# Wide projection fills of the first block queued on TensorE in halves of 12 products instead of whole

## The reference, cut to what matters

```python
h = rmsnorm(x, gain)
u = h @ w_in                      # all projections: q, k, v, z, merge gates
y0 = gated_delta_rule(q, k, v, beta, g)      # GDN, chunks of 64 tokens
y1 = gated_linear_attention(...)             # GLA, 4 heads
y2 = ssd(...)                                # SSD, state-space scan
y3 = sparse_attention(...)                   # NSA: compressed, selected and window keys
for n in range(4):
    y = norm(y_n) * silu(z_n)
    merged += sigmoid(u_gate_n) * (y @ w_br[n])
x = x + merged @ w_out
```

## Time and the profile before

| what | value |
|---|---|
| time, median of 3 runs | 2018.33 us (2018.2 to 2020.39) |
| the profiled execution | 2024.89 us, span 2023.1 us |
| instructions | 28936 |
| mean granted TensorE clock | 0.972 of full speed |
| TensorE busy | 1914.2 us, 95% of the span |
| DVE, ACT, POOL busy | 757.7, 652.8, 543.2 us |
| block one's branches GDN, GLA, SSD, NSA | about 101 to 272, 272 to 490, 490 to 640, 640 to 883 us |
| merge and w_out, block two | 883 to 953, 953 to 2023 us |

### The profile page before, as it was taken

One profiled execution on the slowest core, in us unless ns is written; L12 is line 12 of the kernel. 1 busy time (PEld: TensorE's weight loads), 2 busy tenths in 40 slices (PEclk: granted clock), 3 DMA queues, 4 the chain that ended last, 5 costly groups with the idle time before them and its releaser, 6 DMA issues. The chain is left out here.

```text
span 2023.1 us, 28936 instructions
## 1 busy us (share of the span) xinstructions
PE 1914.2 (95%) x11837; PEld 1438.9 (71%) x11837; DVE 757.7 (37%) x1500; ACT 652.8 (32%) x1251; POOL 543.2 (27%) x420
## 2 busy tenths in 40 slices
PE   6999899998999999999999999999979999999997
PEld 4788877777888777777787887987775444444442
DVE  4367462244322323323434135143242343343333
ACT  4542333232223444435344246343332111111110
POOL 2242233235553433158045230252200000000000
PEclk9999999999899999999999999999989999999999
DMA  5230121124124200252133221232148999999994
GB/s 158 63 88 24 43 73 62 42 63 125 32 63 126 63 22 22 63 194 73 42 123 110 76 81 37 67 102 84 42 201 315 417 413 415 419 418 419 420 420 174
DMA packets 133209, 313.40 MB, mean 155 GB/s; under 512 B 15296, under 2 KB 103120, under 8 KB 108496
## 3 DMA queue, kind: packets, MB, share of 16 engines
q1 hardware_dynamic: 133072, 311.49, 41.3%
HBM read 309.37 MB, written 2.10 MB: 154 GB/s over the span
## 5 line engine op out<-in xcount | busy, mean ns | idle before, releaser
L321 POOL TENSOR_TENSOR unit_low<-unit_ring,unit_high 128x512 fp32r<-128x512 f32 x332 | 437.0, 1342 | 779.2 <-ACT unit_high L314 779.2
L358 PE MATMUL dense<-hT,unit_high 128*128 128x512 f32 x656 | 270.5, 412 | 3.0 <-DVE dense_temps L473 1.7
L359 PE MATMUL dense<-hT,unit_high 128*128 128x512 f32 x656 | 260.4, 397 | 0.0
L360 PE MATMUL dense<-hT,unit_low 128*128 128x512 f32 x656 | 259.8, 396 | 0.0
L396 PE MATMUL dense<-unit_high,hT 128*128 128x256 f32 x832 | 242.5, 291 | 0.4 <-POOL unit_low L321 0.4
L397 PE MATMUL dense<-unit_low,hT 128*128 128x256 f32 x832 | 237.6, 286 | 0.0
L398 PE MATMUL dense<-unit_high,hT 128*128 128x256 f32 x832 | 237.5, 286 | 0.0
L314 ACT CAST unit_high<-unit_ring 128x512 fp32r<-128x512 f32 x332 | 185.8, 620 | 57.3 <-PE dense L360 28.3
L396 PEld LDWEIGHTS dense<-unit_high,hT 128*128 128x128 f32 x832 | 161.9, 195 | 8.0 <-ACT mix_v L2785 3.0
L397 PEld LDWEIGHTS dense<-unit_low,hT 128*128 128x128 f32 x832 | 161.9, 195 | 0.9 <-issue 0.7
L398 PEld LDWEIGHTS dense<-unit_high,hT 128*128 128x128 f32 x832 | 161.7, 194 | 0.0
(11 more groups left out here) (578 smaller groups left out, 3218.0 us busy)
## 6 DMA issues: line engine op xcount, KB each, us to landing
expert_ring<-w_exp_gate SPq DMA_DIRECT2D x64, 1024.0 KB, 9.7
expert_ring<-w_exp_up SPq DMA_DIRECT2D x64, 1024.0 KB, 10.5
expert_ring<-w_exp_down SPq DMA_DIRECT2D x64, 1024.0 KB, 9.0
unit_ring<-w_in SPq DMA_DIRECT2D x55, 1024.0 KB, 5.3
unit_ring<-w_br SPq DMA_DIRECT2D x16, 512.0 KB, 6.3
unit_ring<-w_mkv SPq DMA_DIRECT2D x8, 1024.0 KB, 5.4
x<-x SPq DMA_DIRECT2D x8, 512.0 KB, 4.8
w_out_raw<-w_out SPq DMA_DIRECT2D x4, 1024.0 KB, 10.0
```

Of the source, the lines that this page charges most:

```text
L321: nc.gpsimd.tensor_tensor(low[:, at:at + 512], raw[:, at:at + 512], high[:, at:at + 512], ALU.subtract).then_inc(*self.split.up())
L358: nc.tensor.matmul(out, high[:, k, c], rh, start=(k == 0), stop=False)
L359: nc.tensor.matmul(out, high[:, k, c], rl, start=False, stop=False)
L360: last = nc.tensor.matmul(out, low[:, k, c], rh, start=False, stop=(k == kd - 1))
```

## The change

The fills of block one, and the one kind of block two that shares `dense_z`, yield in the middle: `channels_by_half` after 4 of 8 slices (12 products of 512 columns), `tokens_by_half` after the first of the bank's two token tiles (24 products of 256 columns). Merge products (12) stay whole. `weave` counts in halves: what is due grows by twice `counts[i]` behind each narrow step, half of what is due (rounded up) is issued there, and the rest is carried to the next steps. Everywhere else `fill(dense)` advances to the end of a fill as `next(dense)` did. Casts and evacuation are still issued after the fill's last product. No product, copy or DMA is added or left out; only the order changes (and ACT has two more loads of its function table, in GDN's scores). TensorE's wide work then stands in 165 runs between narrow products instead of 147.

```diff
+    def channels_by_half(self, n, part, col, src, kd=KD, after=None):
...
+        self.round_rest(n)
...
+        for ks in (range(kd // 2), range(kd // 2, kd)):
+            @self.core.section.tensor
+            def _(pe):
+                if ks.start == 0:
+                    if self.free[b]:
+                        pe.wait_ge(*self.free[b])
...
+                for k in ks:
+                    if col == 0:
+                        pe.wait_ge(*self.ready[n, part, k])
...
+                if ks.stop == kd:
+                    last.then_inc(*self.filled.up())
+            if ks.start == 0:
+                yield HALF
+        return self.bank[b], self.filled.now(), b
...
     for c in range(2):
-        got = ring.channels(n, 0, c * P, S.hT)
+        got = yield from ring.channels_by_half(n, 0, c * P, S.hT)
...
-            got = ring.tokens(n, (2 * f, 2 * f + 1), S.hT)
+            got = yield from ring.tokens_by_half(n, (2 * f, 2 * f + 1), S.hT)
...
-                next(dense)
+                fill(dense)
...
+def fill(fills, *over):
+
+    while next(fills, *over) == HALF:
+        pass
+
+
 def weave(steps, fills, counts):
 
+    due, begun = 0, False
     for i, _ in enumerate(steps):
-        for _ in range(counts[i] if i < len(counts) else 0):
-            next(fills, None)
+        due += 2 * counts[i] if i < len(counts) else 0
+        now = (due + 1) // 2
+        while now > 0:
+            half = next(fills, None) == HALF
+            size = 1 if half or begun else 2
+            begun, now, due = half, now - size, due - size
```

More of the change, by code:

```diff
@@ L227, in band_of @@
     return table[:, at:at + n]
+HALF = "half"
 def placed(core, name, offset, shape, dt=F32):
@@ L362, in channels @@
         return self.fill(emit, after)
+    def channels_by_half(self, n, part, col, src, kd=KD, after=None):
+        nc = self.core.nc
+        self.round_rest(n)
+        high, low = self.parts(n, part)
+        b = self.fills % 2
+        self.fills += 1
+        out, c = self.bank[b][:], slice(col, col + P)
+        for ks in (range(kd // 2), range(kd // 2, kd)):
[4 more added lines that the diff above has]
+                        pe.wait_ge(*self.free[b])
+                    if after:
+                        pe.wait_ge(*after)
+                for k in ks:
+                    if col == 0:
+                        pe.wait_ge(*self.ready[n, part, k])
+                    rh, rl = src[:, 0, k, :], src[:, 1, k, :]
+                    nc.tensor.matmul(out, high[:, k, c], rh, start=(k == 0), stop=False)
+                    nc.tensor.matmul(out, high[:, k, c], rl, start=False, stop=False)
+                    last = nc.tensor.matmul(out, low[:, k, c], rh, start=False, stop=(k == kd - 1))
+                if ks.stop == kd:
[3 more added lines that the diff above has]
+        return self.bank[b], self.filled.now(), b
@@ new lines, in tokens_by_half, with _ @@
+    def tokens_by_half(self, n, tiles, src):
+        nc = self.core.nc
+        self.round_rest(n)
+        high, low = self.parts(n, 0)
+        b = self.fills % 2
+        self.fills += 1
+        for i, t in enumerate(tiles):
+            @self.core.section.tensor
+            def _(pe):
+                if i == 0 and self.free[b]:
+                    pe.wait_ge(*self.free[b])
+                out, s = self.bank[b][:, i * 256:(i + 1) * 256], slice(t * P, (t + 1) * P)
+                for k in range(KD):
+                    if t == 0:
+                        pe.wait_ge(*self.ready[n, 0, k])
+                    nc.tensor.matmul(out, src[:, 0, k, s], high[:, k, :], start=(k == 0), stop=False)
+                    nc.tensor.matmul(out, src[:, 0, k, s], low[:, k, :], start=False, stop=False)
+                    last = nc.tensor.matmul(out, src[:, 1, k, s], high[:, k, :], start=False, stop=(k == KD - 1))
+                if i == 1:
+                    last.then_inc(*self.filled.up())
+            if i == 0:
+                yield HALF
+        return self.bank[b], self.filled.now(), b
@@ L550, in dense_merge @@
             chunk = 2 * i + c
-            gate = ring.channels(unit, 0, c * P, S.hT)
+            gate = yield from ring.channels_by_half(unit, 0, c * P, S.hT)
             ring.round(3)
@@ L1627, in dense_ssd_x @@
     for i in range(2):
-        for _ in dense_conv(core, ring, S, f"ssd_x{i}", taps, bias, 2 * i, lambda c: xT[:, c, :], temps, False):
+        for got in dense_conv(core, ring, S, f"ssd_x{i}", taps, bias, 2 * i, lambda c: xT[:, c, :], temps, False):
+            if got == HALF:
+                yield HALF
+                continue
             if chunk >= 1:
@@ L1638, in turn @@
         _, S.ssd_ready = turn_chunk(core, S, bT[:, g, :], S.chunk["ssd_b", g], Bt[:, :, g * P:(g + 1) * P])
[L1639 to L1640 removed]
+    yield from dense_conv(core, ring, S, "ssd_b", taps, bias, 4, lambda c: bT[:, c, :], temps, False)
     turn(0)
[L1642 to L1643 removed]
+    yield from dense_conv(core, ring, S, "ssd_c", taps, bias, 6, lambda c: cT[:, c, :], temps, False)
     turn(1)
@@ L1684, in dense_nsa_kv @@
         n = ring.at[name]
-        got = ring.channels(n, 0, 0, S.hT)
+        got = yield from ring.channels_by_half(n, 0, 0, S.hT)
         ring.round(2)
@@ L1688, in dense_nsa_kv @@
         yield
-        got = ring.channels(n, 0, P, S.hT)
+        got = yield from ring.channels_by_half(n, 0, P, S.hT)
         ring.round(2)
@@ L2442, in blocks @@
         for i in range(8):
-            next(inputs)
+            fill(inputs)
             next(delta)
@@ L2575, in blocks @@
         for i, (k, half) in enumerate(pieces):
-            next(dense, None)
+            fill(dense, None)
             cols = slice(half * SEQ, (half + 1) * SEQ)
```

## The result

The changed kernel takes 2031.2 us (median of 4, 2029.97 to 2031.87), the kernel before 2018.26 us (median of 4): 12.9 us slower, ratio 1.007 with a 95% interval of 1.0048 to 1.0092. The forecast was 2011.8 us, faster; the time lies outside the range, on the other side.

A forecast was written before the change was run, and what follows sets the result against it. TensorE, busy 95% of the span, bounds the kernel, so only its gaps and clock can win. GDN +3.7, GLA +3.1, NSA +1.5 and switches -1.8 make 6.5 us off 2018.3: 2011.8 us, range 2003 to 2020.5.

The forecast's parts named there:

- The step that failed: Closing condition for being wrong: ScalarE's casts, issued later, might leave fills waiting for weights; counted at nothing.
- Nothing to tell: Rival: waits only move and GLA's clock stays low; 0.6 us gained, 2017.7 us; chance 0.25.
- The slower rival: Shorter wide blocks in NSA lower its clock from 0.97 to 0.92, costing 12.2 us; 2024.0 us; chance 0.12.
- GDN, the last tile's state: A half now stands ahead of the state's read, covering its wait of 1.55 us: +1.6 us.
- GDN, the wait for a ring bank: Turnings between halves shorten the 1.7 us wait for a bank the convolution reads: +0.7 us, bounds 0 and +1.7.
- GDN, v and the first inversions: Halves cover up to 2.8 us of waits, less 1.1 new behind the last z evacuation: +1.7, bounds 0 and +2.8.
- GDN, the first solve: Only a half now covers the scaling before the first solve: -0.3 us, from 0 to 1.7 lost.
- GLA, the factors of the last tile: The 3.51 us stall falls to about 0.3, as the tanh moves behind ScalarE's copies: +3.2 us, or +2.1.
- GLA, the clock behind the stall: Without the last tile's stall, the low clock in the fill after it goes: +1.6 us, bounds 0 and +1.6.
- GLA, the new wait: SSD's second turning of B waits behind GLA's last outputs for VectorE's state update, 1.4 to 1.9 us: -1.7.
- NSA: Four of 16 waits for the softmax's maximum get a half in front: +1.5 us, upper bound +4.2.
- Switches: Each of 18 additional pieces of wide work costs 0.1 us: -1.8 us, bounds 0 and -3.6.

The follow-up runs named there:

- casts at the half: Changed kernel with the next unit's casts issued between a fill's two halves instead of after the second, everywhere; 2014.74 us against 2018.04 for the kernel before.
- the two pairs of casts mended: Changed kernel with only two pairs of GDN's casts put back ahead of the exponentials, between the halves; 2017.88 us against 2019.28 for the kernel before.
- the swap in GLA: On casts at the half, the fourth fill ahead of GLA's weave moved behind the turning of the first tile's factors; 2021.29 us, 1.0016 of the kernel before.
- whole fills with late casts: Kernel before, with two pairs of GDN's casts issued one narrow step later, behind the exponentials; 2036.63 us, ratio 1.0093 to the kernel before.
- GDN's table: On casts at the half, GDN's halves set by hand ahead of its waits; 2005.15 us against 2018.55 for the kernel before, ratio 0.9935.

## Why the prediction was wrong

**The step that failed** is the one named last and counted at nothing: "if ACT's casts, now issued later, leave fills waiting for their weights [...] for which I have counted nothing". The rival *Nothing to tell* had it again as "the casts of the next unit now start later", as an argument and without a price. I had shown on ScalarE's order what the change does to a tanh that stands ahead of copies, and did not ask the same of the casts that move with it. In GDN it cost 3.99 + 3.87 = 7.9 us of waits, and the stage went from one stretch of 3.4 us at 1.2 GHz to five of some 24 us together; in all 15.2 us of the stage, by the run with casts at the half. The chain could be read from the order: casts behind L828, L828 behind VectorE's decays, these behind the scores, and between the scores and the product that needs the casts only half a fill and twelve products of the next, 4.4 us.

**The slower rival was the wrong one.** It put the loss in NSA by the clock. NSA's clock stayed at 0.97, with 32 pieces of wide work for 22. The clock did matter, but in GDN, above all at two waits of 4 us.

**GDN, the last tile's state:** +1.6 forecast, 4.7 to 3.1 us measured. Right.

**GDN, the wait for a ring bank:** +0.7 forecast, 1.7 to 0.8 us measured. Right.

**GDN, v and the first inversions:** +1.7 forecast. The waits of 1.2 and 1.6 us went, a new one of 2.3 us came, where I had 1.1: about 0.5 us is left. The mechanism, a gate evacuation ahead of the weighing, was right, its price too low by half.

**GDN, the first solve:** -0.3 forecast, no wait in the changed kernel, 1.8 us with casts at the half, 0.6 with the two pairs of casts mended; so within the bounds of 0 and 1.7 or just beyond. As reckoned, the scaling's operation of 1.79 us took 0.69 in the changed kernel, where no cast runs beside it.

**GLA, the factors of the last tile:** +3.2 forecast; the line went from 7.7 to 4.3 us, this stall from 3.51 to 0.23. Right. But 4.1 us, 1.4 each, for the other three was a wrong reading of a row of totals. The longest, 3.6 us, was not this stall but the one at the first tile, which the change left at 3.6, and the two between were 0.3 each:

```profile
302.06 0.42 PE L1351 MATMUL core<-ident,factors 128*64 128x128 f32 x1 [3.61 <-ACT factorsT L1358]
```

**GLA, the clock behind the stall:** +1.6 forecast, 0 measured. The low stretch at 419 us went, and one of the same length came at 449 us, right behind the new wait:

```profile
449.05 1.00 PE L1667 MATMUL core<-ident,ssd_BT 128*128 128x128 f32 x4 [1.32 <-DVE state L1478]
```

**GLA, the new wait:** -1.7 forecast, 1.32 us measured, in the place and on the operation named. Right, a little under its bounds of 1.4 to 1.9, but for the clock behind it.

**NSA:** +1.5 forecast, 8.4 to 7.7 us measured, in 12 waits as forecast ("some twelve waits"). The four that went are the four counted (0.56, 0.38, 0.28 and 0.26, together 1.5 us), but two others grew by 0.35 and 0.42 us, from 0.29 and 0.51 us in the kernel before:

```profile
776.71 0.49 PE L1870 MATMUL core<-nsa_kwT,nsa_qT 64*128 64x256 f32 x2 [0.29 <-DVE neg_max L1881]
838.85 0.30 PE L1870 MATMUL core<-kcmpT,nsa_qT 64*128 64x31 f32 x2 [0.51 <-DVE neg_max L1881]
```

to 0.64 and 0.93 us in the changed kernel:

```profile
786.67 0.49 PE L1930 MATMUL core<-nsa_kwT,nsa_qT 64*128 64x256 f32 x2 [0.64 <-DVE neg_max L1941]
851.05 0.30 PE L1930 MATMUL core<-kcmpT,nsa_qT 64*128 64x31 f32 x2 [0.93 <-DVE neg_max L1941]
```

Each of these two stands one or two narrow steps behind a half that the change put among the steps. So part of what was covered seems to have been passed on to a later wait, as the rival *Nothing to tell* had it in its words ("Waits only move"); no run takes this apart.

**Switches:** -1.8 forecast. NSA has ten more pieces and lost 0.7 us of waits, and its window is 0.5 shorter, so ten pieces cost 0.2 us; both profiles have the same 13.6 us at 1.2 GHz in the stage. Nearly nothing, not 0.1 to 0.2 each. The row of 2.95 us shows a surplus of 0.2 at a piece's edges; that narrow products among themselves pay only half of it stood in no row. The Trainium skill's rule ("TensorE: Matmul & The Clock Gate", Part 2: What happens when you issue a matmul), that weight loads are pulled ahead of running products, which I had set aside, fits these windows better than my price did. Why a switch is so cheap no run shows.

With the two pairs of casts mended and nothing else, the kernel has the ratio 0.9989 (0.9981 to 0.9998), so it gains 2.2 us, between 0.4 and 3.8. The direction would then have been right and the 6.5 us still too much. GLA's clock (1.6), v's region (1.2) and NSA (0.8) were priced too high, the switches (1.8) too dear the other way; these terms alone would leave 4.5 us or so, and what takes the rest is not shown.

## What to carry to other kernels

When work is cut into pieces, list everything that is issued at the end of a whole piece (casts for the next one, evacuation, release of a buffer), and ask of each what now stands ahead of it in its engine's queue; here the pieces themselves cost next to nothing, and two pairs of casts that moved with them made the kernel 13 us slower. Issue the preparation of the next unit at the first cut, not at the last. Then set the pieces by the waits of the profile: in GDN, a half ahead of most of the waits of 1 to 2 us gave 13 us over the kernel before (9 to 18 by the interval), where the even distribution, with its casts mended, gave 2 to 3. Before moving one fill to free one wait, look for what that fill was hiding: the swap in GLA took a stall of 3.6 us away and brought waits of 6.3 and 3.9 us.

## What the runs showed of the hardware

A wait cost more than its length through the clock. At each of the waits of 3.9 to 6.8 us in GDN (the changed kernel, halves in GDN alone, whole fills with late casts) TensorE fell to 1.2 GHz 0.9 to 4 us before the wait was over, and stayed there for 6.8 us, once for 10.2. Of shorter waits this can't be said: 1.32 us at 449 us of the changed kernel had 3.4 us at 1.2 GHz behind it; the wait of 2.3 us for `delta_v` had 3.4 us behind it in the changed kernel and none with the two pairs of casts mended, where the whole stage is at 1.00. Where GDN's table took 6.9 us of open time away, the stage became 9.2 us shorter. Single executions of the kernel before differ by up to 0.8% in one set (2008.8 to 2025.2 us), and their mean clocks with them (0.982 to 0.970). Its two profiles have the same waits to 0.1 us and differ in how many stretches at 1.2 GHz they have: such a stretch comes or doesn't. A change worth 2 us needs a dozen runs here, and still may not be told.
